# Middle expert rounds of ScalarE and VectorE as loops, gate-row products ahead of a wait, and products of constants in waits: two transformer blocks with routed experts

## The reference, cut to what matters

```python
eid = expert_id.reshape(A)                      # A = 512 pairs of token and expert
order = jnp.argsort(eid)
counts = jnp.bincount(eid, length=MOE_EXPERTS)
...
def expert_block(args):
    xb, e = args
    return (jax.nn.silu(xb @ w_gate[e]) * (xb @ w_up[e])) @ w_down[e]
...
x = x + g1 * y_lat
f_lat = _modulate(x, norm_ffn_g[i], sh2, sc2)
y = _hier_moe(f_lat.reshape(B * S, D), *moe_args)
x = x + g2 * y.reshape(B, S, D)
```

## Time and profile before

| what | value |
|---|---|
| median of three runs | 2103.68 us |
| the profiled execution: time / span | 2106.74 us / 2104.9 us |
| mean granted TensorE clock of it | 0.974 |
| busy: PE, DVE, ACT, POOL | 94%, 47%, 33%, 4% |
| chain that ended last: PE, DMA, DVE, ACT | 71%, 22%, 3%, 2% |
| HBM read, written | 605.09 MB, 25.43 MB |
| layer 0: first quarter product / rounds / norm's transposes done | 1004.50 us / 16 / 1473.70 us |
| layer 1: first quarter product | 1626.10 us |

### The profile page before, as it was taken

How to read it: one execution, slowest core, us unless ns; L and a number is a source line. 1 busy time by engine, 2 the same in 40 slices (tenths; PEclk the granted TensorE clock), 3 DMA queues, 4 the chain that set the end, 5 groups by cost and what they waited for, 6 DMA issues and landing times.

```text
span 2104.9 us, 29466 instructions
## 1 busy us (share of the span) xinstructions
PE 1980.6 (94%) x9665; PEld 1067.4 (51%) x9666; DVE 997.5 (47%) x2226; ACT 686.3 (33%) x1107; POOL 74.4 (4%) x109
## 2 busy tenths in 40 slices
PE   8899999999999999998999898899999999889887
PEld 4536776645577775555333333334775333333333
DVE  2566886303488544445444333335225443334335
ACT  1351000013400002142555444445203554444444
POOL 2000000000000000000000000001000000000001
PEclk9999999999999999999999999999999999999999
DMA  9506999733189543314899999998555999999995
GB/s 307 214 1 264 364 346 378 268 120 142 64 350 364 188 163 125 142 41 179 353 410 421 416 417 422 421 422 356 222 196 204 400 420 422 421 422 421 422 418 233
DMA packets 81567, 623.99 MB, mean 296 GB/s; under 512 B 11548, under 2 KB 11916, under 8 KB 18624
## 3 DMA queue, kind: packets, MB, share of 16 engines
q1 hardware_dynamic: 67968, 540.51, 63.9%
q0 software_dynamic: 10112, 69.67, 8.8%
q10 hardware_dynamic: 3392, 12.68, 1.7%
HBM read 605.09 MB, written 25.43 MB: 300 GB/s over the span
## 4 chain that ended last, share of the span: by engine, by line
PE 71%; DMA 22%; DVE 3%; ACT 2%; issue 1%; ACTq 1%; SPq 0%; DVEq 0%; POOL 0%; POOLq 0%
PE ps L873 26%; DMA big<-in_w_up 21%; PE ps L1329 16%; PE ps L1135 14%; PE ps L1147 7%; PE ps L1295 3%; PE ps L887 2%; PE ps L1331 2%; ACT big L1881 1%; ACTq L1829 1%; PE ps L1313 1%; DMA big<-in_dense 0%; PE ps L1157 0%; ACT big L1796 0%; SPq L798 0%
## 5 line engine op out<-in xcount | busy, mean ns | idle before, releaser
L1329 PE MATMUL ps<-big,hT 128*32 128x512 f32 x3072 | 704.1, 613 | 67.6 <-ACT big L1881 61.8
L1331 PE MATMUL ps<-big,hT 128*32 x1536 | 703.3, 613 | 0.0
L1881 ACT COPY big<-big 128x1024 f32 x384 | 396.2, 1045 | 471.4 <-PE ps L1331 294.6
L2651 DVE TENSOR_SCALAR big<-big 128x1024 f32 x384 | 262.6, 691 | 406.9 <-PE ps L1331 304.6
L1329 PEld LDWEIGHTS ps<-big,hT 128*32 128x32 f32 x3072 | 189.6, 112 | 459.3 <-issue 262.1
L1135 PE MATMUL ps<-hT,big 128*128 128x256 f32 x1408 | 311.2, 379 | 0.0
L873 PE MATMUL ps<-big,hT 128*128 128x512 f32 (+5 forms) x800 | 302.1, 528 | 2.9 <-DMA big<-in_dense 1.3
L1135 PEld LDWEIGHTS ps<-hT,big 128*128 128x128 f32 x1408 | 266.7, 190 | 49.4 <-issue 15.2
L873 PEld LDWEIGHTS ps<-big,hT 128*128 128x128 f32 x800 | 141.6, 191 | 128.8 <-issue 118.1
L1147 PE MATMUL ps<-big 128*128 128x512 f32 x352 | 162.1, 604 | 4.1 <-DVE big L2408 4.1
L1331 PEld LDWEIGHTS ps<-big,hT 128*32 128x32 f32 x1536 | 159.6, 112 | 3.9
(11 more groups left out here) (346 smaller groups left out, 1273.5 us busy)
## 6 DMA issues: line engine op xcount, KB each, us to landing
big<-in_w_gate SPq DMA_DIRECT2D x128, 1024.0 KB, 22.5
big<-in_w_up SPq DMA_DIRECT2D x128, 1024.0 KB, 22.0
big<-in_w_down SPq DMA_DIRECT2D x128, 1024.0 KB, 20.6
big<-in_dense SPq DMA_DIRECT2D x52, 1536.0 KB, 9.1
big<-in_dense POOLq DMA_DIRECT2D x28, 2048.0 KB, 10.2
big<-in_dense SPq DMA_DIRECT2D x20, 2048.0 KB, 8.3
y_rows<-big ACTq DMA_DIRECT2D x2, 6144.0 KB, 58.0
big<-in_dense SPq DMA_DIRECT2D x7, 1024.0 KB, 30.5
```

The costliest lines, as they stand in the source:

```text
L1329: nc.tensor.matmul(ps[g * SLOTS:(g + 1) * SLOTS, bank, :], xT[:, k, g * SLOTS:(g + 1) * SLOTS], side[:, g - 1, quarter % 2, at:at + BW], s ...
L1331: return nc.tensor.matmul(ps[0:SLOTS, bank, :], xT[:, k, 0:SLOTS], experts3[:, bass.ds(here, 1), kind * CH + row:kind * CH + row + BW] .re ...
L1881: nc.scalar.copy(side[:, 1, quarter % 2, :], experts3[:, bass.ds(there, 1), lo:lo + QW] .rearrange("p a n -> p (a n)")).then_inc(s["side2_ ...
L2651: ts(side[:, 0, quarter % 2, :], experts3[:, bass.ds(there, 1), lo:lo + QW].rearrange("p a n -> p (a n)"), 1.0, None, mult).then_inc(s["si ...
```

## The change

1. **Loops.** ACT runs rounds 1 to 14 as a loop (rounds 0 and 15 written out), DVE rounds 2 to 14 (0, 1 and 15 written out). Wait values and addresses now come from registers. All value loads of a round stand at its head: four on DVE, one on ACT. The picks no longer read column b of `rel` but a small tile `rel_now` of 128x4, copied once from `dst_f` at the end of the route and lowered by 32 slots x 3 in each round (`next_round`, behind copy 2).
2. **Gate rows.** PE's two gate-row products stand at the end of `entry`, ahead of the wait for `zdiag`; the wait for `turned_a` that stood ahead of them is dropped.
3. **Products of constants.** `warm(bank, n)` issues n products `ones` x `causal` of 128x256 into a bank that nobody reads: 3 + 3 around the four tiny products of the route (each layer), 4 + 4 around `token_scales` between the layers.

```diff
@@ PE
+            def warm(bank, n):
+
+                for _ in range(n):
+                    nc.tensor.matmul(ps[:, bank, 0:2 * P], const["ones"][:], const["causal"][:], start=True, stop=True)
...
                 logits(4)
+                g2 = st["g2_" + tag]
+                pe.wait_ge(g2["gate_diags"].sem, g2["gate_diags"].end)
+                for h in range(2):
+                    mm(ps[:, 7 - h, :], const["ones"][:], diag2[:, 4 * h:4 * h + 4, :], True, True, g2["gate_ready"].sem)
                 pe.wait_ge(e["zdiag_done"].sem, e["zdiag_done"].end)
...
-                pe.wait_ge(g2["gate_diags"].sem, g2["gate_diags"].end)
-                pe.wait_ge(e["turned_a"].sem, e["turned_a"].end)
-                for h in range(2):
-                    mm(ps[:, 7 - h, :], const["ones"][:], diag2[:, 4 * h:4 * h + 4, :], True, True, g2["gate_ready"].sem)
                 pe.wait_ge(s["route_dve"].sem, s["route_dve"].at(4))
...
                 pe.wait_ge(e["z_copied"].sem, e["z_copied"].end)
+                warm(4, 3)
                 pe.wait_ge(s["route_dve"].sem, s["route_dve"].at(6))
                 for i in range(4):
                     mm(ps[0:1, 5, i * 64:i * 64 + NB], rt[0:E, 3, i:i + 1], past[0:E, :], True, True,
                        s["route_pe"].sem if i == 3 else None)
+                warm(4, 3)
...
+            warm(3, 4)
             token_scales(s, 2)
+            warm(3, 4)
@@ ACT, experts
+                def turn(b, last=False):
+                    there = third(b)
+                    rows_T(b)
+                    copy(b, there, 0)
+                    copy(b, there, 1)
+                    rest_of(b, there, last=last)
...
+                rest_of(0, there, first=True)
+                with act.Fori(1, ROUNDS - 1) as b:
+                    turn(b)
+                turn(ROUNDS - 1, last=True)
@@ DVE, experts
+            def next_round(s, b):
+
+                v.wait_ge(s["pick_ready"].sem, s["pick_ready"].at(b * TC + TC))
+                ts(rel_now, rel_now, -float(ROWS), None, add).then_inc(s["pick_step"].sem, 1)
+                v.wait_ge(s["pick_step"].sem, s["pick_step"].at(b * (TC + 1) + (TC + 1)))
...
-                def turn(b, there, loads):
-                    first, last, following = b == 0, b == ROUNDS - 1, (None, None)
+                def turn(b, first=False, last=False, second_round=False):
+                    there = second(b)
+                    loads = [0, 16, 16] if first else [loads_of(b, q) for q in range(BPE)]
                     for j in range(8):
                         copy(b, there, loads, j, first)
...
+                        if j == 2 and not last:
+                            next_round(s, b)
...
-                    if not last:
-                        then, ahead = second(b + 1), [loads_of(b + 1, 0)]
                     for h in range(2):
                         v.wait_ge(s["hT_ready"].sem, s["hT_ready"].at(b * 2 + (h + 1)))
...
                     if not last:
                         row_half(s, b + 1)
-                        ahead += [loads_of(b + 1, q) for q in range(1, BPE)]
-                        following = then, ahead
...
-                for b in range(ROUNDS):
-                    if b == 1:
-                        after(v, "g2_" + name[-1])
-                    values = turn(b, *values)
+                turn(0, first=True)
+                after(v, "g2_" + name[-1])
+                turn(1, second_round=True)
+                with v.Fori(2, ROUNDS - 1) as b:
+                    turn(b)
+                turn(ROUNDS - 1, last=True)
```

More of the change, by code:

```diff
@@ L416, in two_blocks @@
         slot_i = area(18920, ROUNDS).bitcast(i32)
+        rel_now = area(18936, 2 * TC)
         RB = 3 * CH
@@ L1863, in rows_T, with silu @@
                             .then_inc(s["xT_done"].sem, 1)
-                def silu(b):
+                def silu(b, first=False):
                     act.wait_ge(done.sem, done.at(b * 12 + 4))
-                    if b:
+                    if not first:
                         act.wait_ge(s["hidden_done"].sem, s["hidden_done"].at(b))
@@ L1871, in third, with copy @@
                 def third(b):
-                    return act.value_load(tab_i[0:1, 0, b * WIDE + 2:b * WIDE + 3], min_val=0, max_val=BPE - 1)
-                def copy(b, there, j):
+                    return act.value_load(tab_i[0:1, 0, bass.ds(b * WIDE + 2, 1)], min_val=0, max_val=BPE - 1)
+                def copy(b, there, j, first=False):
                     kind, quarter = j // 4, j % 4
                     if quarter % 2 == 0:
-                        act.wait_ge(s["half_landed"].sem, s["half_landed"].at(6 * b + 2 * kind + quarter // 2 + 1))
-                    if b or j >= 2:
+                        act.wait_ge(s["half_landed"].sem, s["half_landed"].at(b * 6 + (2 * kind + quarter // 2 + 1)))
+                    if not first or j >= 2:
                         act.wait_ge(done.sem, done.at(b * 12 + j - 1))
@@ L1886, in row_half, with rest_of @@
                     nc.scalar.copy(xe[0:ROWS, 0:BW], ps[0:ROWS, 0, :]).then_inc(s["rows_copied_a"].sem, 1)
+                def rest_of(b, there, first=False, last=False):
+                    for j in range(2, 6):
+                        copy(b, there, j, first)
+                    silu(b, first)
+                    for j in range(6, 10):
+                        copy(b, there, j, first)
+                    if not last:
+                        row_half(b + 1)
+                    for j in range(10, 12):
+                        copy(b, there, j, first)
+                def turn(b, last=False):
[4 more added lines that the diff above has]
+                    rest_of(b, there, last=last)
                 after(act, "route" + name[-1])
@@ L1890, in experts @@
                 row_half(0)
-                copy(0, there, 0)
+                copy(0, there, 0, True)
                 rows_T(0, (0,))
-                copy(0, there, 1)
+                copy(0, there, 1, True)
                 rows_T(0, (1,))
-                for b in range(ROUNDS):
[L1896 to L1900, removed]
-                    for j in range(6, 10):
-                        copy(b, there, j)
-                    here = there
-                    if b + 1 < ROUNDS:
-                        row_half(b + 1)
-                        there = third(b + 1)
-                    for j in range(10, 12):
-                        copy(b, here, j)
-                    if b + 1 < ROUNDS:
-                        rows_T(b + 1)
-                        copy(b + 1, there, 0)
-                        copy(b + 1, there, 1)
+                rest_of(0, there, first=True)
+                with act.Fori(1, ROUNDS - 1) as b:
+                    turn(b)
+                turn(ROUNDS - 1, last=True)
             def entry(o_name, tag):
@@ L2652, in copy, with rows_out @@
                        1.0, None, mult).then_inc(s["side1_copied"].sem, 1)
-                def rows_out(b):
+                def rows_out(b, first=False):
                     v.wait_ge(done.sem, done.at(b * 12 + 12))
-                    if b:
+                    if not first:
                         v.wait_ge(s["y_stored"].sem, s["y_stored"].at(b * 16))
@@ L2723, in turn @@
                             add_rows(0, j - 10)
-                    return following
                 def add_rows(c, k):
@@ L2744, in last_picks @@
                     tt(onehot_w[:, 0], onehot_w[:, 0], onehot_w[:, 1], add).then_inc(m["weights_picked"].sem, 1)
-                values = second(0), [0, 16, 16]
-                for b in range(ROUNDS):
-                    if b == 1:
-                        after(v, "g2_" + name[-1])
-                    values = turn(b, *values)
+                turn(0, first=True)
[4 more added lines that the diff above has]
+                turn(ROUNDS - 1, last=True)
                 v.wait_ge(m["last_turned"].sem, m["last_turned"].end)
```

25 lines of the change are left out of this document (13 added, 12 removed).

## The result

The changed kernel takes 2084.78 us (median of four runs, 2080.9 to 2087.33) where the kernel before takes 2105.16 (four runs, 2102.7 to 2106.82): the ratio is 0.9909, 95% interval [0.9896, 0.9922]. The forecast was 2095 with a range down to 2089.5. The direction was right and the size was not: about 9 us were forecast and 20 came. Most of the rest came from the two expert stages, to which the prediction gave nothing: VectorE and ScalarE, looped, fetch few instructions there, and the stream of weights is no longer delayed by those fetches.

The account below looks back on a forecast made before the run. The weight stream's restart and speed, then PE's last 40 us, set the end. Terms -4.3 - 3.95 - 1.2 + 0.3 = -9.15 us gave 2097.6 profiled, 2095 as median; own range 2089.5 to 2100, 2089.5 to 2104.5 leaving out at most 2 in 10.

Parts of the forecast that it names:

- Gate rows: Route, each layer: gate rows fill PE's idle time before z, z runs at full clock, counts start earlier; 2.3 us gained.
- Constants in the route: Route, around the tiny products: constants keep PE's clock up for the row products; 2.6 less 0.6 us gained per layer.
- the rival of a fallen clock: Six short products do not hold the clock, row products stay slow; 3.4 us gained in all, 2100.3 us; chance 14%.
- Passing on: Route to layer's end: gains of 4.3 and 3.95 us, below the stream's holes of 6.6 and 5, all reach the end.
- The rival in which the stream does not start earlier: The stream, not round 0, sets the restart; only the norm's 1.2 us would be left, 2102.5 us; chance 10%.
- the hole in the stream: Weight loads stop once per layer before round 0's quarters; 6.6 us in layer 0, at least 5 in layer 1.
- Constants in the norm: Between the layers: constants fill two PE waits so the first 20 records run at full clock; 1.2 us gained.
- Loops, the head: Round borders: value loads cost 0.7 us per PE-paced loop pass, mostly hidden by the stream; 0.3 us lost in all.
- The slower rival: ACT's and DVE's loops: each jump back fetches instructions again; at 4.3 us a round, 2140 us; chance 12%.
- Loops, fewer fetches: Expert rounds: fewer instructions of DVE and the others fetched, at most 0.4 us gained, taken as none.

Follow-up runs that it names:

- PE's part alone: The kernel before with the gate rows ahead of z and the `warm` products, ACT's and DVE's rounds still written out: 2095.28 us, ratio 0.9954.

## Why the prediction was wrong

The waits before the rounds came as forecast; the term of the fetched instructions was set to nothing and was worth 6.7 to 9.5 us, close to half of the gain.

- **Gate rows** (2.3 us per route): 2.9 to 3.0 measured. z at full clock and the counts behind the picks, as said; 0.7 more, since with the gate rows moved the row products take 4.87 us for 5.44 and wait 0.3 us less. The prediction had not seen that.
- **Constants in the route** (2.0 per layer): 1.4. That the two together came to 4.3 and 4.2 us, as forecast, is luck: one term was 0.7 too small and the other 0.6 too large. The clock was 1.00 over the row products, so the rival of a fallen clock is out.
- **Passing on**: all of it arrives at the end; PE's part alone gives 9.7 us by the ratio, and its routes and norm 9.5 in the profile. The rival in which the stream does not start earlier is out. SP's restart moved from 1008.80 to 1004.03. The 1004.6 us from which the prediction measured the hole in the stream is a slip: the last packet of weights ends at 1004.2, and the hole is 7.0 us and not 6.6, which changes nothing.
- **Constants in the norm** (1.2): 0.8 to 1.0, in a stretch that itself varies by more.
- **Loops, the head** (0.7 per border, mostly hidden): 0.9 and 1.2 in the rounds that PE sets, and hidden as said: the rounds got shorter for all that. The slower rival, a fetch at each jump back, is out: between 1060 and 1420 us the changed kernel has not one instruction packet,

```profile
q1 hardware_dynamic: 20573, 149.82, 99.9%
q0 software_dynamic: 1456, 1.88, 1.4%
```

and DVE's branch takes 0.056 us in the trace where I had priced it at PE's 0.22. The Trainium skill's rule ("Runtime: NRT & Kernel Launch", section on instruction fetch mechanics: a jump to a target outside the pages held forces a fetch) is neither borne out nor contradicted: DVE's loop has 86 instructions and ACT's 55, neither shows a fetch at its jump back, and no run here has a loop that does.
- **Loops, fewer fetches: the step that failed.** "Fewer instructions are fetched; the fetches [...] were 0.09 MB, 0.1% of the DMA time [...], so at most 0.4 us, and I take none." The share is a mean over 16 engines, and I read a limit for the whole stream out of it; on one engine the same 11 packets of 0.31 to 0.33 us would be 3.5 us. In its place: behind a DVE packet that the trace shows as 0.33 us long the lag of the slowest engine steps up by about 1 us, in layer 1 six times in a row, and each load waits for that engine. The gain was 6.7 us alone and 9.5 beside the rest, and not 0. The Trainium skill ("DMA: Bandwidth & Descriptors", section "Why a DMA increments its semaphore by 16 and not by 1") has a load over 128 partitions split over 16 engines; the share of 0.06 agrees with that.

Shown: that fetched instructions of DVE, and not executed ones, cost this time, taken away and added. Shown by the windows and landings: that one engine is late when they are fetched. Inferred from the steps alone: that DVE's packets all ride on that one engine. Not shown: why a packet of 0.33 us costs 1 us, on which engines the packets of ACT and PE lie, how ACT's and PE's packets cost their 5 and 6 us, and what sets the 2 to 4 us by which the rounds of equal lists differ between executions. No version here beats the changed kernel.

## What to carry to other kernels

Where a stage is bound by a stream of bulk loads, try short instruction lists beside it: loop them, on every engine. Here VectorE's loop was worth 10 us, TensorE's 6 and ScalarE's 5. Never price a small transfer by its share of 16 engines; ask what it does to the one engine that it rides on, and look at the end of the stream for a share of 0.06. And a loop can afford a somewhat longer head where the stream sets the pace: 1.2 us more at each of 30 borders cost 4 to 6 us and not 36.

## What the runs showed of the hardware

- DVE's and ACT's instructions come in packets of 8 KB (queue q14) of 0.31 to 0.34 us, PE's in packets of 16 KB (q8) that take some 1.0 us each. A PE loop of 164 products per pass, an ACT loop of 55 instructions and DVE loops of 86 and of 134 (86 and 48) run without being fetched again.
- With DVE's instructions fetched, bulk loads at 420 GB/s leave the sixteen engines unevenly loaded: 9 us between the mean and the last at the end of layer 1 in the kernel before, over 10 with more instructions, and 3 to 4.5 with DVE looped.
